# The second FFN's up projection as seven half-size products per pair of tiles, with the weight sums added in DRAM

## The reference, cut to what matters

```python
def swiglu(xn, w_gate, w_up, w_down):
    return (jax.nn.silu(xn @ w_gate) * (xn @ w_up)) @ w_down
```

## Time and profile before

| | |
|---|---|
| median of 3 runs | 2182.81 us |
| profiled execution: span from first to last instruction | 2180.8 us |
| what lies around the span in the median run | 2.0 us |
| PE busy | 2163.9 us, 99% |
| DVE, ACT, POOL busy | 1270.0, 922.8, 477.5 us |
| HBM read | 183.77 MB |
| granted TensorE clock | 1.00 |

### The profile page before, as it was taken

How to read it: one execution, slowest core, us unless ns; L and a number is a source line. 1 busy time by engine, 2 the same in 40 slices (tenths; PEclk the granted TensorE clock), 3 DMA queues, 4 the chain that set the end, 5 groups by cost and what they waited for, 6 DMA issues and landing times.

```text
span 2180.8 us, 27395 instructions
## 1 busy us (share of the span) xinstructions
PE 2163.9 (99%) x10292; PEld 1782.4 (82%) x10292; DVE 1270.0 (58%) x2127; ACT 922.8 (42%) x1651; POOL 477.5 (22%) x357
## 2 busy tenths in 40 slices
PE   9999999999999999999999999999999999999998
PEld 6777898888888888888887888888887778888887
DVE  7778334677486584866776434434557774424244
ACT  6776433436432222245775322222446763322223
POOL 1000521243311010163672110101232211101002
PEclk9999999999999999999999999999999999999999
DMA  6232211222233233232112232332323213344332
GB/s 193 88 106 59 96 49 53 74 87 69 97 97 97 97 97 97 90 100 92 59 57 69 92 99 95 97 101 91 99 92 89 81 59 93 108 119 116 97 97 97
DMA packets 87716, 198.66 MB, mean 91 GB/s; under 512 B 32160, under 2 KB 36512, under 8 KB 87584
## 3 DMA queue, kind: packets, MB, share of 16 engines
...
HBM read 183.77 MB, written 6.82 MB: 87 GB/s over the span
## 4 chain that ended last, share of the span: by engine, by line
PE 92%; DVE 3%; ACT 2%; issue 1%; POOLq 0%; DVEq 0%; POOL 0%; DMA 0%; SPq 0%; ACTq 0%
PE bank L362 16%; PE bank L363 16%; PE bank L366 16%; PE bank L435 8%; PE bank L438 8%; PE bank L436 8%; PE bank L385 2%; PE bank L384 2%; PE bank L386 2%; PE bank L1983 1%; PE bank L1253 1%; PE bank L2010 1%; PE bank L2009 1%; PE bank L1630 1%; PE bank L1296 1%
## 5 line engine op out<-in xcount | busy, mean ns | idle before, releaser
L270 ACT ACTIVATE b_wh<-b_raw 128x1024 fp32r<-128x1024 f32 (+1 forms) x329 | 341.3, 1038 | 993.8 <-PE bank L366 698.3
L288 DVE TENSOR_TENSOR b_wl<-b_raw,b_wh 128x1024 fp32r<-128x1024 f32 (+2 forms) x286 | 351.5, 1229 | 169.6 <-ACT b_wh L270 169.1
L362 PE MATMUL bank<-b_xh,b_wh 128*128 128x512 f32 x1080 | 421.3, 390 | 0.0
L363 PE MATMUL bank<-b_xl,b_wh 128*128 128x512 f32 x1080 | 420.3, 389 | 0.0
L366 PE MATMUL bank<-b_xh,b_wl 128*128 128x512 f32 x1072 | 417.4, 389 | 0.0
L672 POOL TENSOR_TENSOR b_yl<-b_arena,b_yh 128x512 fp32r<-128x512 f32 x66 | 115.6, 1751 | 867.6 <-ACT b_yh L647 867.6
L435 PE MATMUL bank<-b_xh,b_wh 128*128 128x512 f32 x712 | 295.2, 415 | 0.4 <-DVE b_wl L288 0.4
L436 PE MATMUL bank<-b_xl,b_wh 128*128 128x512 f32 x712 | 278.0, 390 | 0.0
L438 PE MATMUL bank<-b_xh,b_wl 128*128 128x512 f32 x704 | 276.0, 392 | 0.0
L362 PEld LDWEIGHTS bank<-b_xh,b_wh 128*128 128x128 f32 x1080 | 202.7, 188 | 43.6 <-issue 0.4
L363 PEld LDWEIGHTS bank<-b_xl,b_wh 128*128 128x128 f32 x1080 | 202.8, 188 | 41.2
...
## 6 DMA issues: line engine op xcount, KB each, us to landing
b_raw<-in_zga SPq DMA_DIRECT2D x16, 512.0 KB, 3.6
b_raw<-in_c0up SPq DMA_DIRECT2D x16, 512.0 KB, 3.5
b_raw<-in_c1up SPq DMA_DIRECT2D x16, 512.0 KB, 3.4
b_raw<-in_fqk SPq DMA_DIRECT2D x16, 512.0 KB, 3.5
b_raw<-in_s0up SPq DMA_DIRECT2D x16, 512.0 KB, 3.5
b_raw<-in_s1up SPq DMA_DIRECT2D x16, 512.0 KB, 3.5
b_raw<-in_m0up SPq DMA_DIRECT2D x16, 512.0 KB, 3.5
b_raw<-in_m1up SPq DMA_DIRECT2D x16, 512.0 KB, 4.0
```

The costliest lines, as they stand in the source:

```text
L270: act.activation(wh[:, par, cols], raw[:, par, cols], ACT.Copy).then_inc(w_hi, 1)
L288: dve.tensor_tensor(wl[:, par, cols], raw[:, par, cols], wh[:, par, cols].bitcast(F32), ALU.subtract).then_inc(w_lo, 1)
L362: pe.matmul(bank[:, :], ph[:, w], hi[:, x, :], start=(k == 0), stop=False)
L363: last = pe.matmul(bank[:, :], ph[:, w], lo[:, x, :], start=False, stop=(n in SIDE_BY_SIDE and k == kt - 1))
```

## The change

Of the 22 pairs the first 4 stay as they are (`s0up`, now 8 panels). The other 18 are done in seven products of half the size each way: the contraction is cut in two halves of 4 slices, the tokens in two halves of 256, and gate and value are the two halves of the output. Seven products of (128 x 512) by (512 x 256) replace eight. The operands are sums: four of the seven weight factors are sums of the quarters g0, v0, g1, v1 (gate and value, first and second half of the contraction), and the seven factors of x are sums and differences of its quarters.

- The sums of weights are made on the chip: 32 DMAs from POOL's queue (`move_sum`), DRAM to DRAM, 16 of them accumulating, for groups of 4, 4, 4 and 6 pairs (1 MB and 1.5 MB a DMA), each waiting for the one before. 22 are issued in the first FFN, ahead of each pair's low part, and 10 at the starts of heads 0 to 9 of the FoX stage.
- A panel in the new segments `s0st`, `s1st`, `s2st` holds two factors of 128 x 512 side by side, loaded in two DMAs of 256 KB. There are 14, 28 and 21 panels, 3.5 a pair. The buffers and their number stay.
- The seven operands of x, with high and low parts, are made during `s0up` by VectorE, ScalarE and POOL (`halves_dve`, `halves_act`, `halves_pool`); they hold the norm already.
- `seven_pe` uses banks 2, 3, 4, 5, 2, 4, 5 for the products; products 4, 5 and 6 add to what their bank holds. VectorE makes two more sums and the outputs (`seven_dve`), ScalarE the copy of product 0 and the Silus (`seven_act`). The sine at the second chunk moves ahead of the segment's first panel copy.

The other edits only rename or carry tables through (a panel's buffer, the count that its load must reach, five semaphores of an earlier stage used again, the layout of the quarters in DRAM). The diff, cut:

```diff
         ("fv0", 4, 8), ("ff", 1, 8), ("fv1", 4, 8), ("fqk", 16, 8), ("fo", 8, 8),
-        ("s0up", 16, 8), ("s0dn", 8, 8), ("s1up", 16, 8), ("s1dn", 8, 8), ("s2up", 12, 8), ("s2dn", 8, 6),
+        ("s0up", 8, 8), ("s0st", 14, 8), ("s0dn", 8, 8), ("s1st", 28, 8), ("s1dn", 8, 8), ("s2st", 21, 8), ("s2dn", 8, 6),
...
+SEVEN = {"s0st": (0, 4, 4, 0), "s1st": (1, 0, 8, 4), "s2st": (2, 0, 6, 12)}
...
+QUARTERS = ["g0", "v0", "g1", "v1"]
+SUMS = ["g0+v0+v1", "g0+v0", "v1+v0", "g0+v0+v1+g1"]
+FACTORS = ["g0", "g0+v0+v1", "g0+v0", "v1+v0", "g1", "v1", "g0+v0+v1+g1"]
+
+MOVES = [("g0+v0", "v0"), ("v1+v0", "v1"), ("g0+v0", "g0"), ("v1+v0", "v0"),
+         ("g0+v0+v1", "g0+v0"), ("g0+v0+v1", "v1"), ("g0+v0+v1+g1", "g0+v0+v1"), ("g0+v0+v1+g1", "g1")]
+PIECES = [(0, 4), (4, 4), (8, 4), (12, 6)]
...
+        def move_sum(pool, i):
+
+            a, cnt = PIECES[i // len(MOVES)]
+            to, of = MOVES[i % len(MOVES)]
+
+            def rows(name):
+                src = I["quarters"][QUARTERS.index(name)] if name in QUARTERS else sums[SUMS.index(name)]
+                return src[a:a + cnt].rearrange("n p k -> (n p k)").rearrange("(r c) -> r c", c=4 * T)
+            wait(pool, s_sums, 16 * i)
+            added = i % len(MOVES) in (2, 3, 5, 7)
+            pool.dma_start(rows(to), rows(of), max_dma_last_dim=8192,
+                           accum_op=ALU.add if added else ALU.bypass).then_inc(s_sums, 16)
+
+        def seven_load(sp, seg):
+
+            _, _, pairs, before = SEVEN[seg]
+            for i in range(CNT[seg]):
+                n = BASE[seg] + i
+                buffer_free(sp, n, w_lo)
+                for half in range(2):
+                    j = 2 * i + half
+                    p, name = before + j // 7, FACTORS[j % 7]
+                    if name in SUMS:
+                        piece = [a <= p < a + c for a, c in PIECES].index(True)
+                        sp.wait_ge(s_sums, 16 * len(MOVES) * (piece + 1))
+                    src = I["quarters"][QUARTERS.index(name), p] if name in QUARTERS else sums[SUMS.index(name), p]
+                    sp.dma_start(raw_of(n)[:, half * T:half * T + T], src).then_inc(w_raw[BUFFER[n]], 16)
+
...
+        def seven_pe(pe, seg):
+
+            _, _, pairs, before = SEVEN[seg]
+            for j in range(7 * pairs):
+                n, half, i, p = BASE[seg] + j // 2, j % 2, j % 7, before + j // 7
+                if half == 0:
+                    pe.wait_ge(w_lo, n + 1)
+                if p == 0:
+                    if i in (0, 4, 6):
+                        pe.wait_ge(xs_lo_pool, xs_pool0 + (0, 4, 6).index(i) + 1)
+                    else:
+                        pe.wait_ge(xs_lo_done, xs_lo0 + (1, 2, 3, 5).index(i) + 1)
+                if i == 0:
+                    wait(pe, gate0_read, p)
+                if i == 2:
+                    wait(pe, quarter_read, 4 * p - 1)
+                if i == 3:
+                    wait(pe, quarter_read, 4 * p)
+                if i == 4:
+                    pe.wait_ge(p1_copied, p1_0 + p + 1)
+                if i in (5, 6):
+                    pe.wait_ge(quarter_read, 4 * p + i - 4)
+                bank = pb[SEVEN_BANK[i]][:, 0:T // 2]
+                ph, pl = panel_hi_lo(n)
+                for k in range(4):
+                    w = slice(half * T + k * P, half * T + k * P + P)
+                    pe.matmul(bank, ph[:, w], xs_hi[i][:, k, :], start=(i < 4 and k == 0), stop=False,
+                              skip_group_check=(i > 3))
+                    pe.matmul(bank, ph[:, w], xs_lo[i][:, k, :], start=False, stop=False,
+                              skip_group_check=(i > 3))
+                    m = pe.matmul(bank, pl[:, w], xs_hi[i][:, k, :], start=False, stop=(k == 3),
+                                  skip_group_check=(i > 3))
+                m.then_inc(mm_done if half else even_done, 1)
+
...
+        def seven_dve(dve, seg):
+
+            ch, q0, pairs, before = SEVEN[seg]
+            hidden0 = HIDDEN_BEFORE[seg[0]] + PAIRS[ch][0] + q0
+
+            def quarter(i):
+                return pb[SEVEN_BANK[i]][:, 0:T // 2]
+
+            def gated(q):
+                dve.wait_ge(gate_silu, hidden0 + q + 1)
+                wait(dve, y_ready, YR[seg[0]] + PAIRS[ch][0] + q0 + q)
+                dve.scalar_tensor_tensor(out=pr, in0=vt, scalar=-1.0, in1=gt, op0=ALU.mult, op1=ALU.mult)\
+                    .then_inc(prod_done, 1)
+            for j in range(7 * pairs):
+                n, q, i = BASE[seg] + j // 2, j // 7, j % 7
+                p = before + q
+                if i == 0 and q > 0:
+                    gated(q - 1)
+                if i in (1, 2, 3, 5, 6):
+                    product_done(dve, seg, j)
+                if i == 1:
+                    dve.wait_ge(p1_copied, p1_0 + p + 1)
+                    dve.tensor_tensor(un, quarter(1), p1, ALU.subtract).then_inc(out_free, 3 + p % 2)
+                    dve.drain()
+                if i == 2:
+                    dve.tensor_tensor(tmp, quarter(2), un, ALU.subtract).then_inc(quarter_read, 1)
+                    dve.drain()
+                if i == 3:
+                    dve.tensor_tensor(vt[:, T // 2:T], quarter(3), tmp, ALU.add).then_inc(quarter_read, 1)
+                if i == 5:
+                    dve.tensor_tensor(vt[:, 0:T // 2], quarter(5), un, ALU.subtract).then_inc(quarter_read, 1)
+                if i == 6:
+                    dve.tensor_tensor(tmp, quarter(6), un, ALU.subtract).then_inc(quarter_read, 1)
+                    dve.drain()
+                if j % 2 == 0:
+                    split_lo(dve, n + 2, 0, n % 2, KT_OF[n + 2])
+            gated(pairs - 1)
+
...
+        def seven_act(act, seg):
+
+            ch, q0, pairs, before = SEVEN[seg]
+            hidden0 = HIDDEN_BEFORE[seg[0]] + PAIRS[ch][0] + q0
+
+            def gate1(q):
+                act.wait_ge(quarter_read, 4 * (before + q) + 4)
+                act.activation(gt[:, T // 2:T], tmp, ACT.Silu).then_inc(gate_silu, 1)
+
+            def product_hi(q):
+                act.wait_ge(prod_done, hidden0 + q + 1)
+                act.activation(yh[:, q0 + q, :], pr, ACT.Copy).then_inc(yh_done, 1)
+            for j in range(7 * pairs):
+                n, q, i = BASE[seg] + j // 2, j // 7, j % 7
+                if j % 2 == 0:
+                    split_hi(act, n + 2, 0, n % 2, KT_OF[n + 2])
+                if i == 0:
+                    if q > 0:
+                        gate1(q - 1)
+                    product_done(act, seg, j)
+                    act.activation(p1, pb[SEVEN_BANK[0]][:, 0:T // 2], ACT.Copy).then_inc(p1_copied, 1)
+                if i == 1 and q > 0:
+                    product_hi(q - 1)
+                if i == 4:
+                    product_done(act, seg, j)
+                    act.wait_ge(prod_done, hidden0 + q)
+                    act.activation(gt[:, 0:T // 2], pb[SEVEN_BANK[4]][:, 0:T // 2], ACT.Silu).then_inc(gate0_read, 1)
+            gate1(pairs - 1)
+            product_hi(pairs - 1)
...
+            def step(t):
+                if t < 2:
+                    for k in range(3 * t, 3 * t + 3):
+                        x(k)
+                if t == 2:
+                    x(6)
+                    x(7)
+                    dve.drain()
+                    add(xs[2], xs[6], x10, ALU.subtract)
+                    dve.drain()
+                if t == 3:
+                    add(xs[3], xs[0], x10, ALU.subtract)
+                    add(xs[1], xs[0], xs[2], ALU.add)
+                    dve.drain()
+                if t == 4:
+                    add(xs[5], xs[1], xs[4], ALU.subtract)
+                    dve.drain()
+                    lo(1)
+                if t == 5:
+                    lo(2)
+                    lo(3)
+                if t == 6:
+                    lo(5)
...
+        def halves_act(act):
+
+            order, need = (0, 4, 6, 2, 3, 1, 5), (4, 8, 8, 9, 10, 11, 12)
+
+            def split(c):
+                act.wait_ge(xs_raw, xs_raw0 + need[c])
+                act.activation(xs_hi[order[c]], xs[order[c]], ACT.Copy).then_inc(xs_split, 1)
+            at = {2: (0,), 3: (1, 2), 4: (3, 4, 5), 5: (6,)}
+            return {t: lambda t=t: [split(c) for c in at[t]] for t in at}
+
+        def halves_pool(pool):
+
+            pool.wait_ge(xs_raw, xs_raw0 + 12)
+            for c, i in enumerate((0, 4, 6)):
+                pool.wait_ge(xs_split, xs_split0 + c + 1)
+                pool.tensor_tensor(xs_lo[i], xs[i], xs_hi[i].bitcast(F32), ALU.subtract).then_inc(xs_lo_pool, 1)
...
+        def hidden_pool(pool, l, ch, beside={}):
             first, cnt = PAIRS[ch]
 
             def body(q):
+                if q in beside:
+                    beside[q]()
                 pool.wait_ge(yh_done, q + (YH[l] + first + 1))
                 pool.tensor_tensor(tile_of(yl, q), pr, tile_of(yh, q).bitcast(F32), ALU.subtract).then_inc(y_ready, 1)
...
             for ch in range(3):
```

(66 more changed lines are left out.)

62 lines of the change are left out of this document (38 added, 24 removed).

## The result

The changed kernel takes 2244.53 us (median of 4 runs, 2242.5 to 2245.77) against 2182.88 for the kernel before (2182.62 to 2182.95): a ratio of 1.028, 95% interval 1.0266 to 1.0295, or 61.7 us more. The forecast was 2195.3, with a range up to 2216. The profiled run took 2242.5 us, its span is 59.6 us longer than the one before.

A forecast was written before the change was run, and what follows sets the result against it. TensorE's own pace bounds the kernel before; the chain of load, copy, subtraction and gate was to pace the half-size stage. + 2.5 - 1.9 + 5.7 + 3.2 + 3 = + 12.5 us on 2182.8 gives 2195.3 us, range 2177 to 2216.

The forecast's parts named there:

- the moves in DRAM: 32 DMAs on POOL's queue: nothing late in the first FFN, none to 30 us in the heads, 3 us taken.
- Rival 3: FoX heads: adding DMAs at three times a copy make POOL's subtractions late, costing 20 to 30 us, about 2220; chance 0.15.
- The halves of x: making x's operands beside seven 5.44 us panels, 3 us of slack each, lags up to 2 us; counted as nothing.
- The pitch: half-size stage: 256-wide matmuls start 0.1175 us apart (bounds 0.111 and 0.12); eighteen pairs gain 18.2 us if nothing else bounds.
- The cycle: half-size stage: seven panels (two pairs) take 22.05 us; nine cycles 198.4 us, 2.5 more than today's 195.9.
- the hole: head of s1st: the rope angles on VectorE delay the sine, copy and subtraction for panel 2; 5.7 us, once.
- the panels prepared beforehand: head of each of the three half-size stretches: two panels are ready early, worth 0.6 us each, - 1.9 in all.
- The down joints: start of the down projections: the last hidden tile comes after TensorE needs it, costing 0.6 + 0.6 + 2.0 = 3.2 us.
- Rivals 1 and 2: half-size stage, faster loads: TensorE stays the bound, 2173.5 to about 2179 (chance 0.18); or level, 2183 (chance 0.17).

The follow-up runs named there:

- the last kernel: the base with four buffers for the half-size panels, ScalarE's bank reads first and the rope angles spread over the down projection: 2172.84 us.
- the base: the changed kernel with all 32 moves in the first FFN and all seven low parts of x's halves subtracted on VectorE: 2195.4 us.

## Why the prediction was wrong

- **The step that failed is the moves in DRAM.** I took 3 us out of 0 to 30, and it is 41.2, all in the heads. I let a move hold POOL only where the next move waits for it, "4 to 5 us each, four times". But each is followed by a drain in `project_pool`, and this drain holds POOL until the move has landed. Ten times 6.5 to 11.7 us (8.4 and 6.9 for the two of 1 MB) stood, in place of drains of 2.5, on an engine whose next operand each head needs. I had asked what POOL waits for before it issues a move, and not what stands behind the move on its queue.
- **Rival 3** had the right place and the wrong mechanism. It was to decide only from 2.5 times a copy on; an add of 1.5 MB lands after 11.3 us to 6.7 in the median, that is 1.7 times, and still costs 24 us with the one of 1 MB, with another 17 for the plain waits. Its 20 to 30 are too low, so the range was too. Its arithmetic slipped besides: twice the 7.8 us of a copy is 15.6 and not 13.8, three times is 23.4 and not 21.
- **The halves of x** were counted at nothing for a cover of 3 us a panel. The cover was there; the price of the work wasn't the one of rows 3 and 8, because two engines subtract side by side. Measured: 5.9 us, gone when one engine does it all.
- **The pitch** of 0.1175 measured 0.120, my upper bound: 63 x 24 x 0.0025 = 3.8 us of TensorE's gain, unseen here since the stage was bound otherwise, and real in the last kernel, whose three stretches take 182.9 us, 13.0 less than before, where I had 18.2.
- **The cycle** of 22.05 us was right in size (21.5 to 22.7). The two halves of a panel have landed 3.3 us after the first issue in the median, for my 3.5, but in the base five of 63 take 4.75 or more. The three stretches exceed the forecast by 4.5 us: 2.3 for the cycles without the hole, nearly all of it the one of 24.5 with its late loads, 0.2 for the cycle with the hole, and 1.9 that I had taken off for the panels prepared beforehand and that don't show. What I had wrong was to treat the cycle as one sum: from it a load 0.5 us faster saved 1.5 a cycle, and half the bytes saved 0.6.
- **The hole** was to cost 5.7 us. It is 5.5 beyond the pitch, and 7.3 with the slow matmuls behind it (s1st takes 80.6 us against 87.9, with four buffers).
- **The down joints**: 0.2, 0.2 and 1.0 us, not 0.6, 0.6 and 2.0.
- Rivals 1 and 2 needed the load to land in 3.0 to 3.2. Even with 256 KB a panel, landed after 2.6 us, the cycle stays at 21.45, so neither could have come out by a faster load. The 2.0 us plus bytes over 436 GB/s that the prediction quotes from the Trainium skill ("DMA: Bandwidth & Descriptors", section "Anatomy of one DMA") is a fit for DMAs issued by GpSimd, and SP loads the panels: the 3.05 us estimated from it measured 3.3.

The base without both surprises, 2195.4, is the forecast's number; that its errors cancel there (4.9 too few for the three stretches, 1.8 too many for the down joints, 3 too many for the moves) is chance.
